# Eight more hyena projection tiles with 512-wide products, and a new order of exponentials, normalising and convolutions

## What is computed

```
hn = rmsnorm(x, norm1_g[l]);  proj = hn @ w_in[l]
q, k, v, hy_in, gates = split(proj)            # 512, 512, 512, 1536, 2048 columns
a_out = neighbourhood_attention(rmsnorm(q), rmsnorm(k), v, na_rpb[l])      # 8 heads of 64
u = up[:, :-2] * w[0] + up[:, 1:-1] * w[1] + up[:, 2:] * w[2] + b          # short_conv, up = padded hy_in
b_out = hyena_mixer(u, h_fwd, h_bwd, hy_bias[l])   # x0, x1, v = split(u); z = v*x1; long convolution of z, times x0
merged = sigmoid(gates_0) * (a_out @ w_up_na) + sigmoid(gates_1) * (b_out @ w_up_hy)
x = x + merged @ w_out[l]
x = x + peer(rmsnorm(x, norm2_g[l]), ...)      # 16384 single-neuron experts, top 16 for each of 8 heads
```

## Time and profile before

| what | value |
|---|---|
| median of three runs | 1975.44 us |
| the profiled execution, its own time | 1975.33 us |
| its span, first to last instruction | 1973.5 us |
| PE busy | 1967.4 us (100%) |
| weight loads | 1709.1 us (87%) |
| POOL busy | 1603.0 us (81%) |
| DVE busy | 1268.2 us (64%) |
| ACT busy | 1126.3 us (57%) |
| granted TensorE clock | 1.000 of full speed (2.4 GHz) |

### The profile page before, as it was taken

One profiled execution on the slowest core, in us unless ns is written; L12 is line 12 of the kernel. 1 busy time (PEld: TensorE's weight loads), 2 busy tenths in 40 slices (PEclk: granted clock), 3 DMA queues, 4 the chain that ended last, 5 costly groups with the idle time before them and its releaser, 6 DMA issues.

```text
span 1973.5 us, 41116 instructions
## 1 busy us (share of the span) xinstructions
PE 1967.4 (100%) x11758; PEld 1709.1 (87%) x11758; DVE 1268.2 (64%) x2845; ACT 1126.3 (57%) x2467; POOL 1603.0 (81%) x1314
## 2 busy tenths in 40 slices
PE   9999999999999999999999999999999999999999
PEld 8999888888888888888889998888888888888887
DVE  6887589888886333333379875998888863333333
ACT  6565666655555555555576555666555555555554
POOL 7767979888778888888878688898877888888886
PEclk9999999999999999999999999999999999999999
DMA  8544645554444555555575445455545455555554
GB/s 273 170 144 154 207 159 190 191 177 162 160 160 163 199 193 191 191 192 193 199 223 169 139 162 201 163 190 190 171 159 170 159 170 191 191 192 192 193 194 154
DMA packets 100323, 357.34 MB, mean 181 GB/s; under 512 B 11744, under 2 KB 13730, under 8 KB 99492
## 3 DMA queue, kind: packets, MB, share of 16 engines
q1 hardware_dynamic: 99828, 354.36, 54.1%
q10 hardware_dynamic: 432, 2.18, 0.3%
HBM read 355.45 MB, written 1.05 MB: 181 GB/s over the span
## 4 chain that ended last, share of the span: by engine, by line
PE 93%; DVE 4%; ACT 1%; DMA 0%; issue 0%; SPq 0%; POOL 0%; DVEq 0%; ACTq 0%
PE bank L2214 35%; PE bank L1737 27%; PE bank L1741 13%; PE bank L1719 3%; PE bank L2151 3%; PE bank L1724 1%; PE bank L2075 1%; DVE arena L1270 1%; PE bank L1766 1%; PE bank L2130 1%; DVE arena L1253 1%; PE bank L2090 1%; PE bank L1704 1%; PE bank L1702 1%; PE bank L1700 1%; ACT w_hi L542 1%
## 5 line engine op out<-in xcount | busy, mean ns | idle before, releaser
L472 POOL TENSOR_TENSOR w_lo<-ring,w_hi 128x512 fp32r<-128x512 f32 x1046 | 1401.0, 1356 | 282.1 <-ACT w_hi L542 278.0
L542 ACT ACTIVATE w_hi<-ring 128x512 fp32r<-128x512 f32 x1312 | 752.5, 620 | 164.5 <-PE bank L1724 66.8
L1737 PE MATMUL bank<-act_parts,w_hi 128*128 128x512 f32 x2048 | 712.7, 395 | 0.0
L1741 PE MATMUL bank<-act_parts,w_lo 128*128 128x256 f32 x2048 | 560.7, 277 | 0.0
L472 DVE TENSOR_TENSOR w_lo<-ring,w_hi 128x512 fp32r<-128x512 f32 x258 | 238.1, 923 | 450.6 <-ACT w_hi L542 450.4
L1737 PEld LDWEIGHTS bank<-act_parts,w_hi 128*128 128x128 f32 x2048 | 380.9, 188 | 84.6 <-POOL w_lo L472 0.6
L2214 PE MATMUL bank<-w_hi,e_hi 128*128 128x512 f32 x1020 | 397.1, 389 | 0.0
L2214 PE MATMUL bank<-w_lo,e_hi 128*128 128x512 f32 x1020 | 396.8, 389 | 0.0
L2214 PE MATMUL bank<-w_hi,e_lo 128*128 128x512 f32 x1020 | 396.8, 389 | 0.0
L1741 PEld LDWEIGHTS bank<-act_parts,w_lo 128*128 128x128 f32 x2048 | 384.5, 188 | 3.8
L888 ACT ACTIVATE e_hi<-arena 128x256 fp32r (+1 forms) x256 | 106.7, 418 | 315.9 <-PE bank L2214 315.9
(11 more groups left out here) (291 smaller groups left out, 2342.3 us busy)
## 6 DMA issues: line engine op xcount, KB each, us to landing
ring<-stream SPq DMA_DIRECT2D x654, 512.0 KB, 3.3
arena<-rpb_in SPq DMA_DIRECT2D x8, 512.0 KB, 6.1
arena<-subkeys ACTq DMA_DIRECT2D x2, 1024.0 KB, 5.3
ring<-stream SPq DMA_DIRECT2D x4, 256.0 KB, 4.8
xT<-x_in SPq DMA_DIRECT2D x4, 256.0 KB, 4.8
arena<-w_in SPq DMA_DIRECT2D x2, 512.0 KB
arena<-decay_in SPq DMA_DIRECT2D x2, 512.0 KB
arena<-dft_in SPq DMA_DIRECT2D x2, 512.0 KB, 4.9
```

Source lines behind the costliest of these rows:

```text
L472: eng.tensor_tensor(w_lo[:, part_, :], ring[:, tile % RING, half * HT:(half + 1) * HT], w_hi[:, part_, :].bitcast(F32), ALU.subtract).then ...
L542: nc.scalar.activation(w_hi[:, 2 * (tile % AHEAD) + half, :], ring[:, tile % RING, half * HT:(half + 1) * HT], ACT.Copy).then_inc(hi_ready ...
L1737: return T.matmul(out_[:, 0:2 * S], weights(w_hi, tile, k), both[:, :, k, :], start=(k == 0), stop=mirrored and k == KT - 1, skip_group_ch ...
L1741: return T.matmul(out_[:, 0:S], weights(w_lo, tile, k), both[:, 0, k, :], start=False, stop=not mirrored and k == KT - 1, skip_group_check ...
```

## The change

The eight hyena tiles made by `project` are made as the first four were, by one function `hyena` in place of `both_halves`. Each of them has an ACT copy of the bank's upper half and an add on DVE, and the banks' waits follow: hyena tiles from the fifth on, and gate tiles 0 to 3, wait for DVE's add of four tiles earlier. DVE's list gets eight `add_hyena`. ACT's list takes the exponentials of head 0 ahead of hyena copy 10 (and with it ahead of the splitting of gate tile 0), and those of head 1 ahead of hyena copy 11. On DVE conv 3 moves from its place ahead of normalise 0 to the end of the list, behind normalise 7; conv 4 moves ahead of the loop; and within the loop normalise 2, 4 and 6 are called ahead of a convolution in place of behind it. The order of DVE becomes: add 4, 5, add 6, conv 0, add 7, conv 1, scores 0, 1, add 8, conv 2, add 9, normalise 0, add 10, conv 4, add 11, conv 8, normalise 1, conv 5, scores 2, 3, normalise 2, conv 9, attention_parts 0, conv 6, normalise 3, conv 10, scores 4, 5, normalise 4, conv 7, attention_parts 1, conv 11, normalise 5, scores 6, 7, normalise 6, z, attention_parts 2, normalise 7, conv 3, z_lo. In the output projection the two products of tile 1 are issued ahead of the wait for the last row.

```diff
                 def hyena_in(n):
-                    copy_tile(T_HY + n, 8 + n, u_pad[:, n, 1:S + 1])
+                    tile_wait(T_HY + n)
+                    nc.scalar.activation(u_pad[:, n, 1:S + 1], bank[n % 4][:, S:2 * S], ACT.Copy
+                                         ).then_inc(hyena_low.sem, 1)
...
                 load_table(ACT.Exp)
+                head_exp(0)
                 hyena_in(10)
-                head_exp(0)
+                head_exp(1)
                 hyena_in(11)
-                head_exp(1)
...
                 ins.then_inc(bias_ready.sem, 1)
+                add_hyena(4)
+                add_hyena(5)
...
                 def conv(n):
-                    if n < 4:
-                        dve.wait_ge(hyena_sum.sem, hyena_sum.at(l, n + 1))
-                    else:
-                        dve.wait_ge(tile_copied.sem, tile_copied.at(l, 4 + n + 1))
+                    dve.wait_ge(hyena_sum.sem, hyena_sum.at(l, n + 1))
...
+                add_hyena(6)
                 conv(0)
+                add_hyena(7)
                 conv(1)
                 head_scores(0)
                 head_scores(1)
+                add_hyena(8)
                 conv(2)
-                conv(3)
-                tiles = [4, 8, 5, 9, 6, 10, 7, 11]
+                add_hyena(9)
                 normalise_probs(0)
+                add_hyena(10)
+                conv(4)
+                add_hyena(11)
+                tiles = [8, 5, 9, 6, 10, 7, 11]
...
                         head_scores(2 * p + 3)
+                        normalise_probs(2 * p + 2)
                         if tiles:
                             conv(tiles.pop(0))
                         if p == 2:
                             V.tensor_tensor(zT[:, :, :], u[:, 4:8, :], u[:, 8:12, :], ALU.mult
                                             ).then_inc(z_ready.sem, 1)
-                        normalise_probs(2 * p + 2)
+                conv(3)
...
-                def both_halves(tile, m, used):
-                    if used is not None:
-                        pe.wait_ge(tile_copied.sem, tile_copied.at(l, used))
+                def hyena(n):
+                    tile, m = T_HY + n, 8 + n
+                    if n < 4:
+                        pe.wait_ge(tile_copied.sem, tile_copied.at(l, 5 + n))
+                    else:
+                        pe.wait_ge(hyena_sum.sem, hyena_sum.at(l, n - 3))
...
                 def project(tile, m, wait=None, parts=(act_hi, act_lo)):
-                    if 12 <= m < 16:
+                    if 20 <= m < 24:
                         pe.wait_ge(hyena_sum.sem, hyena_sum.at(l, m - 11))
...
                 for n in range(4, 7):
-                    project(T_HY + n, 8 + n)
+                    hyena(n)
...
-                project(T_HY + 7, 15)
-                project(T_HY + 8, 16)
+                hyena(7)
+                hyena(8)
                 pe.wait_ge(spec_ready.sem, spec_ready.at(l, 2))
                 head_pair(0)
-                project(T_HY + 9, 17)
-                project(T_HY + 10, 18)
-                project(T_HY + 11, 19)
+                hyena(9)
+                hyena(10)
+                hyena(11)
...
                 for k in range(KT):
-                    pe.wait_ge(up_used.sem, up_used.at(l, 8 + k + 1))
                     if k == KT - 1:
                         out_high(1, 0)
                         out_high(1, 1)
+                    pe.wait_ge(up_used.sem, up_used.at(l, 8 + k + 1))
                     out_high(0, k)
                     ins = out_low(0, k)
```

More of the change, by code:

```diff
@@ L295, in encoder_kernel @@
         sin_done = sig("sin_done", 2)
-        tile_copied = sig("tile_copied", 32)
-        hyena_low = sig("hyena_low", 4)
-        hyena_sum = sig("hyena_sum", 4)
+        tile_copied = sig("tile_copied", 24)
+        hyena_low = sig("hyena_low", 12)
+        hyena_sum = sig("hyena_sum", 12)
         q_lo_ready = sig("q_lo_ready", 2 * PH)
@@ L581, in tile_wait @@
                     split_next()
-                def copy_tile(tile, m, dst):
-                    tile_wait(tile)
-                    nc.scalar.activation(dst, bank[m % 4][:, 0:S], ACT.Copy).then_inc(tile_copied.sem, 1)
                 def raw_high(n, k, src):
@@ L739, in act_layer @@
                 for n in range(4):
-                    tile_wait(T_HY + n)
-                    nc.scalar.activation(u_pad[:, n, 1:S + 1], bank[n][:, S:2 * S], ACT.Copy
-                                         ).then_inc(hyena_low.sem, 1)
+                    hyena_in(n)
                 for n in range(4):
@@ L1202, in add_hyena @@
                     dve.wait_ge(hyena_low.sem, hyena_low.at(l, n + 1))
-                    V.tensor_tensor(u_pad[:, n, 1:S + 1], u_pad[:, n, 1:S + 1], bank[n][:, 0:S], ALU.add
+                    V.tensor_tensor(u_pad[:, n, 1:S + 1], u_pad[:, n, 1:S + 1], bank[n % 4][:, 0:S], ALU.add
                                     ).then_inc(hyena_sum.sem, 1)
@@ L1781, in project @@
                 def project(tile, m, wait=None, parts=(act_hi, act_lo)):
-                    if 12 <= m < 16:
+                    if 20 <= m < 24:
                         pe.wait_ge(hyena_sum.sem, hyena_sum.at(l, m - 11))
                     elif m >= 4:
-                        pe.wait_ge(tile_copied.sem, tile_copied.at(l, m - 3 if m < 12 else m - 7))
+                        pe.wait_ge(tile_copied.sem, tile_copied.at(l, m - 3 if m < 20 else m - 15))
                     contract(bank[m % 4][:, 0:S], 0, tile, wait=wait, parts=parts).then_inc(tile_done.sem, 1)
@@ L1924, in pe_layer @@
                         ins.then_inc(ffn_done.sem, 1)
-                both_halves(T_HY, 8, 5)
-                both_halves(T_HY + 1, 9, 6)
+                hyena(0)
+                hyena(1)
                 pe.wait_ge(qk_scale_ready.sem, qk_scale_ready.at(l, 1))
@@ L1931, in pe_layer @@
                 spread_scales()
-                both_halves(T_HY + 2, 10, 7)
-                both_halves(T_HY + 3, 11, 8)
+                hyena(2)
+                hyena(3)
                 pe.wait_ge(sin_done.sem, sin_done.at(l, 2))
@@ L2028, in up @@
                         if m < 4:
-                            pe.wait_ge(tile_copied.sem, tile_copied.at(l, 32))
+                            pe.wait_ge(tile_copied.sem, tile_copied.at(l, 24))
                         else:
```

## The result

The changed kernel took 1984.66 us in the median of its first six runs (1982.26 to 1986.22), the kernel before 1975.33 beside it: a ratio of 1.0043, 95% interval 1.0033 to 1.0053. It is slower, by 9.3 us, and lies above the range of the forecast (1972.2 to 1979.8). The profiled execution's span is 1982.5 us, against 1973.5 before.

What follows compares the result with a forecast made beforehand. PE was taken as the bound (93% of the chain, DVE 4%). Two layers of +1.16 us (wait at head 3) and -0.57 (output projection) gave +1.2 us on 1975.3: 1976.5 us, range 1972.2 to 1979.8.

Steps and rivals of the forecast that it cites:

- Wide tiles: Eight hyena tiles a layer, 2.79 us each, save PE 0.7 us; some 0.6 us reaches the gate tiles.
- Adds: Eight adds on DVE, 0.33 us each, 2.7 a layer, not blocked by POOL; add 7's wait loses 0.45 us.
- Exponentials ahead: Head 0's exponentials ahead of hyena copy 10: gate tile 0's low part still in time, nothing or at worst 0.3 us a layer.
- Odd normalisings: Normalise 1, 3, 5 come 2.85 us later; margins 2.97 at head 1, 1.69 at head 3, so PE loses 1.16 us once.
- What I can't read off is the length of the convolutions: Convolutions in new places on DVE: 2.9 us taken, longer ones about as often as conv 3's loss gives back.
- The upper end: Three more of 24 DVE instructions ahead of normalise 3 fall behind POOL's: 2.7 us more, gate stretch 3.9 later.
- Even heads' 0.5 and tiles' 0.6 swallowed: PE's saved waits at even heads and faster wide tiles bring no gain: both vanish in the wait at head 3.
- Conv 3 last costs nothing: Conv 3 ahead of z_lo fits DVE's 3.20 us wait there: nothing, at worst 0.95 us a layer.
- Out products: Output projection: two products ahead of the wait fill PE's gap, last row's product earlier, -0.57 us a layer.
- DVE becomes the bound: Rival, 14 in 100: DVE passes lateness between pairs of heads; three more blocked instructions a layer, +6.7 us, 1982.
- PE keeps its pace: Rival, 30 in 100: no wait before normalise 3; tiles 0.6, even heads 0.5, output 0.57 a layer; 1972.0 to 1973.2.
- Wide products are much cheaper: Rival, 1 in 100: wide products at 0.13 us instead of 0.230; sixteen tiles save 12.8 us, 1963.

Runs made afterwards that it cites:

- e2: The kernel before with only the changed order of exponentials, normalisings and convolutions, no wide tiles, no adds: 1977.14 us, ratio 1.0008.
- e8: The changed kernel with the exponentials of heads 0 and 1 back behind hyena copies 10 and 11: 1974.56 us, ratio to before 0.9996.
- e1: The changed kernel with conv 4 back in the loop, later convolutions each one slot later on DVE's list: 1972.81 us, ratio to before 0.9989.
- e7: The changed kernel with exponentials of heads 2, 4, 6 behind the next gate tile's splitting and copy on ACT: 1975.36 us, ratio to before 1.0000.
- e5: The changed kernel with POOL's subtractions of the 16 gate tiles cut to 64 of 512 columns (gates' low products wrong): 1972.11 us, ratio to before 0.9985.
- e11: The kernel before with only the exponentials of heads 0 and 1 moved ahead of hyena copies 10 and 11: 1976.00 us, ratio 1.0003.
- e10: The changed kernel with conv 4 in the loop and exponentials of heads 0 and 1 behind copies 10 and 11: 1972.39 us, ratio to before 0.9983.
- e9: The changed kernel with the odd heads' normalising ahead of the first convolution of its loop pass: 1980.02 us, ratio to before 1.0022.
- e3: The kernel before with only the wide tiles and their eight adds, in its old orders: 1985.41 us, ratio 1.0045.

## Why the prediction was wrong

The cause has four parts, and without any one of them most or all of the loss is gone: the eight adds (e2 has all the orders without them, +0.7 us a layer, though without wide tiles too), the early exponentials (e8, +0.2), no slack at the odd heads (conv 4 ahead of the loop, e1, -1.0), and the tie from late scores through ACT's list to POOL's bursts (e7, +0.4), which acts by contention (e5, -1.0). The adds and the exponentials only make the start late. From head 2 on DVE, ACT and POOL work through the same lists in e2, e8 and the changed kernel, and yet e2 and e8 repeat every 15.2 us and the changed kernel every 16.75.

- *Wide tiles:* right. 2.80 us each, gate tile 0 earlier by 0.44 us where I said 0.6.
- *Adds:* the size was right, 0.41 us each beside a busy POOL and none blocked; add 7 waits 0.71 for its copy, where I said 0.45. But "nothing hides them but the margins above" was the whole danger, and I passed over it. That no DVE instruction with a single SBUF input contends, as the prediction puts it, holds for the add and not in general: a convolution's first one (L1243) has one SBUF tensor beside its two columns and takes 0.41 us alone and 1.37 to 1.41 beside POOL.
- *Exponentials ahead, "nothing, or at worst 0.3 us a layer":* the step that failed most. It checked whether PE would get gate tile 0's w_lo in time, and PE did (head 0 has no wait). It didn't ask what the later splitting does to POOL's list: eight subtractions with no gap, and 1.8 us more for convs 4 and 8 than in e8. By e8 and the changed kernel the early exponentials are worth 97.39 - 93.43 = 4.0 us a layer, not 0 to 0.3; by e11, nothing without the rest.
- *Odd normalisings, late by 1.16 us at head 3, once:* wrong in kind. Head 1 was late already, though it was to hold by 2.97 - 2.85, and heads 3 and 5 wait 1.10 each again. I wrote that DVE is "all but full", and still treated 2.97 and 1.69 as slack that is paid once. The 15.09 us period of before against PE's own 14.82 (e1, e5) shows that DVE set the pace already. Whatever makes its instructions longer in a period is then paid in each period.
- *"What I can't read off is the length of the convolutions":* right that this was the open term, wrong value. I took them as unchanged on average; the three lines' means went from 828, 880 and 1048 ns to 1013, 1170 and 950 over all twelve, so a convolution from 2.76 to 3.13 us. The upper end, 3.9 us a layer, was nearly what came.
- *Even heads' 0.5 and tiles' 0.6 swallowed:* they weren't gained, but not for the reason given: the even heads still wait, 0.4 us each, because the whole period is DVE's.
- *Conv 3 last costs nothing:* right. DVE still waits 3.13 us ahead of z_lo in the changed kernel (at 145.25), where the earlier trace rows have 3.20.
- *Out products, -0.57 a layer:* right, 0.56.
- *Rivals:* "DVE becomes the bound" named the mechanism, lateness passed from pair to pair by scores, exponentials and splitting, with 3.9 us a layer against 4.1 found. Its 14 in 100 was too low: I had judged each of its links alone and none as a loop. Its price came near by another sum, though: three more blocked instructions a layer, where the trace has 1.66 us more in every period. "PE keeps its pace" is what e1 and e10 show (1972.4 to 1972.8, forecast 1972.0 to 1973.2), one slot of the convolutions away from the changed kernel; with half of the first two gains its own sum is 1973.1, not 1973.2. "Wide products are much cheaper" is out by the 2.80 us a tile; its sum should have had 8 x (0.240 - 0.13) = 0.88 us a tile, so 14.1 and not 12.8.

Not settled: why the bursts lock in at 3.4 us of waiting on ACT and not at 1.8. Counted from the first product of the stretch, head 2's scores begin after 54.5 us in e8 and 55.0 in e2, which repeat every 15.2 us, and after 56.3 in the changed kernel and e9, which repeat every 16.75 and 16.64. In e7 they begin at 56.3 too, and with the tie gone it repeats every 14.9. No run lies between 55.0 and 56.3.

## What to carry to other kernels

When one engine shows no idle time in a period, and the bounding engine waits for it even 0.3 us each time round, that engine is the pacemaker: a margin elsewhere in the period is not slack, and what lengthens its instructions is paid every time round. For an operation moved on an in-order engine, follow not only who waits for its result but also what was queued behind it, down to when the next engine works and which work of another engine it then holds up: in this kernel four subtractions in a row cost DVE more than the same work in pairs. Where DVE and POOL compete, try each reordering with its neighbours one place to either side, since such orders interact: an edit worth nothing on the kernel before (e11) was worth 8 to 10 us in the changed one (e8).

## What the runs showed of the hardware

A locked pattern of DVE, ACT and POOL holds by itself over the periods of a layer, in both layers. DVE's same work of a period (22 instructions by the windows, 21 in e1's) takes 14.53, 16.19 or 14.29 us (before, changed, e1), by how it falls against POOL's, and 9.50 with POOL's subtractions cut short (e5). With the adds in place, a shift of ACT's work of about 1.2 us at the start of the stretch selects between periods of 15.2 and 16.75 (e8, changed). And PE's clock: 3.56 us without work were followed by 2.8 us at a granted 0.50 in e3, worth 1.4 us more than the wait, while waits of up to 1.10 us (changed kernel) and 1.62 (e9) left the granted clock at 1.00.
